# A decoder layer's merge and last feed forward: the squares, the first root and the first four weights of the feed forward made inside merge, whose last two blocks run chunk by chunk

## What is computed

```python
merged = jax.nn.sigmoid(ga) * (att @ w_branch_attn) + jax.nn.sigmoid(gr) * (rec @ w_branch_hgrn)
x = x + merged @ w_out
x = x + 0.5 * _swiglu(_rms_norm(x, ffn2_norm), ffn2_w_gate, ffn2_w_up, ffn2_w_down)
```

## Time and profile before

| | us |
|---|---|
| median of three runs | 3084.69 |
| the three runs | 3084.69, 3096.48, 3047.57 |
| the profiled execution | 3043.1 |
| its span, first to last instruction | 3041.4 |
| its mean granted TensorE clock | 0.959 |

### The profile page before, as it was taken

How to read it: one execution, slowest core, us unless ns; L and a number is a source line. 1 busy time by engine, 2 the same in 40 slices (tenths; PEclk the granted TensorE clock), 3 DMA queues, 4 the chain that set the end, 5 groups by cost and what they waited for, 6 DMA issues and landing times. The chain is left out here.

```text
span 3041.4 us, 50419 instructions
## 1 busy us (share of the span) xinstructions
PE 2893.8 (95%) x19265; PEld 2801.3 (92%) x19265; DVE 1496.7 (49%) x3238; ACT 701.6 (23%) x1354; POOL 578.4 (19%) x328
## 2 busy tenths in 40 slices
PE   8999999999799995999989989989989999999998
PEld 7999999999699983999968989979979999999998
DVE  5233322223677638999944656657344222333323
ACT  5111111111322225222213444431031111111111
POOL 0122122112221102222131121222002111221220
PEclk9999999999899998999999977889999999999999
DMA  4111111110223211233363142224211111111111
GB/s 128 42 44 61 47 41 55 41 41 21 97 58 96 72 51 44 91 132 114 104 168 87 44 157 69 87 92 144 56 49 56 42 41 41 41 59 51 41 34 58
DMA packets 239559, 213.04 MB, mean 70 GB/s; under 512 B 27106, under 2 KB 216834, under 8 KB 239298
## 3 DMA queue, kind: packets, MB, share of 16 engines
q1 hardware_dynamic: 229122, 180.85, 19.9%
q10 hardware_dynamic: 6336, 18.88, 1.6%
q0 software_dynamic: 3968, 11.54, 1.4%
HBM read 168.00 MB, written 43.21 MB: 69 GB/s over the span
## 5 line engine op out<-in xcount | busy, mean ns | idle before, releaser
L271 POOL TENSOR_TENSOR ff_wlo<-ff_raw,ff_whi 128x1024 fp32r<-128x1024 f32 x124 | 298.4, 2427 | 1203.8 <-ACT ff_whi L369 1202.5
L567 DVE TENSOR_TENSOR ff_prod<-ff_silu,ff_gu 128x384 f32<-128x384 f32 x132 | 68.7, 521 | 806.9 <-ACT ff_silu L374 806.9
L97 PE MATMUL ff_dn<-ff_ahi,ff_whi 128*128 128x384 f32 (+1 forms) x1056 | 341.0, 323 | 5.6 <-DVE ff_alo L573 3.8
L97 PE MATMUL ff_gu<-front_hhi,ff_whi 128*128 128x384 f32 (+1 forms) x1056 | 340.8, 323 | 1.8 <-DVE front_hlo L511 1.5
L98 PE MATMUL ff_dn<-ff_alo,ff_whi 128*128 128x384 f32 (+1 forms) x1056 | 339.7, 322 | 0.0
L99 PE MATMUL ff_dn<-ff_ahi,ff_wlo 128*128 128x384 f32 (+1 forms) x1056 | 339.6, 322 | 0.0
L99 PE MATMUL ff_gu<-front_hhi,ff_wlo 128*128 128x384 f32 (+1 forms) x1056 | 339.4, 321 | 0.0
L98 PE MATMUL ff_gu<-front_hlo,ff_whi 128*128 128x384 f32 (+1 forms) x1056 | 339.4, 321 | 0.0
L97 PE MATMUL ff_gu<-rear_hhi,ff_whi 128*128 128x384 f32 (+1 forms) x1056 | 338.8, 321 | 0.0
L98 PE MATMUL ff_gu<-rear_hlo,ff_whi 128*128 128x384 f32 (+1 forms) x1056 | 338.5, 321 | 0.0
L99 PE MATMUL ff_gu<-rear_hhi,ff_wlo 128*128 128x384 f32 (+1 forms) x1056 | 338.5, 321 | 0.0
(11 more groups left out here) (352 smaller groups left out, 6189.9 us busy)
## 6 DMA issues: line engine op xcount, KB each, us to landing
ff_raw<-in_ffn_w_gate SPq DMA_DIRECT2D x44, 512.0 KB, 3.7
ff_raw<-in_ffn_w_up SPq DMA_DIRECT2D x44, 512.0 KB, 3.7
ff_raw<-in_ffn_w_down SPq DMA_DIRECT2D x44, 512.0 KB, 3.5
scratch_feat<-sel_stage ACTq DMA_DIRECT2D x32, 528.0 KB, 2.7
sel_raw<-in_w_in SPq DMA_DIRECT2D x28, 512.0 KB, 3.6
merge_gates<-scratch_feat SPq DMA_DIRECT2D x48, 176.0 KB, 2.8
tok_raw<-in_w_in SPq DMA_DIRECT2D x8, 1024.0 KB, 6.6
mix_pages<-in_cache_k SPq DMA_DIRECT2D x52, 128.0 KB, 2.5
```

The lines of the kernel that those rows point to most:

```text
L97: nc.tensor.matmul(out, w_hi, x_hi, start=first, stop=False)
L271: nc.gpsimd.tensor_tensor(wlo[:, u, :], raw[:, u % RAW, :], whi[:, u, :], ALU.subtract).then_inc(w_lo_done, 1)
L567: nc.vector.tensor_tensor(prod[:, 0:w], act_out[:, b, 0:w], gu[:, b, 1, 0:w], ALU.mult).then_inc(prod_done, 1)
```

## The change

**Memory.** A new `EndRoom`, made before merge and kept through the feed forward, holds the sums of squares, the gain, and a large tile `branches`. Merge's high and low branch inputs lie in that tile; once the branch products are done, it holds the feed forward's weights and gate products.

**Merge.** After the gate products, SP loads the gain and, one after another, the first four gate and up weights into a part of the gates' room. ScalarE squares each block of `xT` after its additions (`square`), in its loop behind the conversion of the next weights, and then converts one of the four end weights (`end_hi`) in four of the steps. VectorE makes their low parts (`end_lo`). GpSimd adds the squares of blocks 1 to 5 to the sums (`gather`); block 0's squares are written straight into them. The loops of the second half are written out on ScalarE, VectorE and GpSimd. The last two blocks (6 and 7) are taken chunk by chunk: chunk 0 of both, chunk 1 of both, chunk 2 of both. Their squares are added by VectorE (`last_gather`). In front of the last product, TensorE multiplies the finished sums of the feed forward's first chunk with the ones (one product for what were eight), and the root of that chunk is made and refined beside the last product.

**The feed forward.** It starts with the scalings of chunk 0. Chunks 1 and 2 have one product with the ones each, ahead of sixteen idle products. Its loads begin with the fifth weight. The first feed forward (ff1) does the same work as before.

```diff
@@ -111,8 +111,31 @@
 LOGS = "natural_log_exp_and_others"
+class EndRoom:
+    def __init__(self, scope):
+        self.square_sums = scope.sb("square_sums", [P, T])
+        self.root = self.square_sums[:, 0:CHW]
+        self.branches = scope.sb("branches", [P, 16 * T], F32R, align=512)
+        self.gain = scope.sb("end_gain", [P, KD])
+        weights = self.branches[:, 0:12 * UNIT].rearrange("p (a b) -> p a b", b=UNIT)
+        self.whi, self.wlo = weights[:, 0:6, :], weights[:, 6:12, :]
+        a = self.branches[:, 12 * UNIT:12 * UNIT + 4 * TP].rearrange("p (a b) -> p a b", b=TP)
+        self.ahi, self.alo = a[:, 0:2, :], a[:, 2:4, :]
+        self.loaded, self.gain_in = scope.sem("end_loaded"), scope.sem("end_gain_in")
+        self.w_hi_done, self.w_lo_done = scope.sem("end_hi_done"), scope.sem("end_lo_done")
+def gate_or_up(w_gate, w_up, n, u):
+    return (w_gate, w_up)[u % 2][0].rearrange("(k p) f -> p k f", p=P)[:, :, DynSlice((2 * n + u // 2) * P, P)]
 def feed_forward(nc, tag, xT, hhi, hlo, gain, w_gate, w_up, w_down, ident, ones, x_in=None, gain_row=None, next_gain=None,
-                 y_out=None, constants=None, x_out=None):
+                 y_out=None, constants=None, x_out=None, given=None):
@@ -405,16 +434,9 @@
                         hi(0, 4)
                         hi(0, 5)
             else:
-                square(0)
-                inverse_root(0)
-                hi(0, 0)
-                square(1)
-                hi(0, 1)
                 h_hi(0)
-                hi(0, 2)
-                hi(0, 3)
+                nc.scalar.preload_act_table_set(LOGS)
                 inverse_root(1)
-                square(2)
                 h_hi(1)
                 inverse_root(2)
                 silu(0, 0)
@@ -602,20 +624,14 @@
                     for n in range(5 + 2 * q, 7 + 2 * q):
                         keep_y_lo(n)
             else:
-                variance(0)
-                lo(0)
                 dve.wait_ge(gain_in, 16)
-                refine(0)
                 for k in range(KD):
                     scale(0, k)
-                lo(1)
                 h_lo(0, 0)
                 h_lo(0, 1)
-                variance(1)
-                lo(2)
-                lo(3)
+                for e in range(S0, NCH):
+                    variance(e)
                 normalise(1)
-                variance(2)
                 product(0, 0)
                 normalise(2)
                 product(0, 1)
...
-                    pe.wait_ge(squared, KD * (e - E0) + k + 1)
-                    nc.tensor.matmul(out, ones[:, :], sq[:, k % 2, 0:w], start=(k == 0), stop=(k == KD - 1)
-                                     ).then_inc(summed, 1)
+                nc.tensor.matmul(dn[:, 1 + e, 0:w], ones[:, :], given.square_sums[:, cols(e)], start=True, stop=True
+                                 ).then_inc(summed, 1)
             def gate_up(i, q, between=None):
                 c, b = q // 2, q % 2
@@ -790,9 +801,9 @@
                 for q in range(3):
                     gate_up(0, q, rows_between)
             else:
-                idle_products(nc, gu[:, 1, 1, 0:P], ident, 10)
-                for e in range(NCH):
+                for e in range(S0, NCH):
                     sums(e)
+                idle_products(nc, gu[:, 1, 1, 0:P], ident, 16)
                 for q in range(3):
                     gate_up(0, q)
             for q in range(3, QS):
...
     RING = 3
     with Scope(nc, "merge") as s:
-        bhi = s.sb("bhi", [P, 8, T], F32R)
-        blo = s.sb("blo", [P, 8, T], F32R)
+        bhi = end.branches[:, 0:8 * T].rearrange("p (a b) -> p a b", b=T)
+        blo = end.branches[:, 8 * T:16 * T].rearrange("p (a b) -> p a b", b=T)
+        square_sums = end.square_sums
         mhi = s.sb("mhi", [P, KD, T], F32R)
         mlo = s.sb("mlo", [P, KD, T], F32R)
         whi = s.sb("whi", [P, 2, UNIT], F32R)
         wlo = s.sb("wlo", [P, 2, UNIT], F32R)
         branch = s.sb("branch", [P, RING, 2, CH])
-        gates = s.sb("gates", [P, 2, 2, CH])
-        both = s.sb("both", [P, 2, CH])
+        gates_room = s.sb("gates", [P, 3, CH])
@@ -2963,6 +2989,14 @@
                 for y in range(6):
                     load_gates(i, y)
+            sp.wait_ge(ps_done, 24)
+            sp.wait_ge(gated, 48)
+            sp.dma_start(end.gain[:, :], end_gain).then_inc(end.gain_in, 16)
+            for u in range(4):
+                if u:
+                    sp.wait_ge(end.w_lo_done, u)
+                sp.dma_start(end_raw.rearrange("p (k f) -> p k f", k=KD), gate_or_up(w_gate, w_up, 0, u)).then_inc(end.loaded, 16)
         @block.gpsimd
         def _(pool):
             s.clear_retired(pool)
...
                     else:
-                        pool.dma_start(raw[:, u, :].rearrange("p (k f) -> p k f", k=KD), wo[:, :, DynSlice((2 * i + u) * P, P)]
+                        pool.dma_start(raw[:, u, :].rearrange("p (k f) -> p k f", k=KD), wo[:, :, (2 * i + u) * P:(2 * i + u + 1) * P]
                                        ).then_inc(w_loaded[u], 16)
-            pairs(pool, body)
+                        if 2 * i + u >= 5:
+                            gather(2 * i + u - 4)
+            def gather(m):
+                for c in range(NCH):
+                    n = NCH * (m - 1) + c
+                    acc = square_sums[:, c * CH:(c + 1) * CH]
+                    pool.wait_ge(squared, n + NCH + 1)
+                    if n >= NCH:
+                        pool.wait_ge(gathered, n - NCH + 1)
+                    nc.gpsimd.tensor_tensor(acc, acc, squares[:, n % SQUARES, :], ALU.add).then_inc(gathered, 1)
+            body(0, 0, 0, True)
+            with pool.Fori(1, 4) as i:
+                body(0, i, i, False)
+            for i in range(4):
+                body(1, i, i + 4, False)
+            gather(4)
+            gather(5)
         @block.scalar
         def _(act):
             def hi(u):
                 nc.scalar.activation(whi[:, u, :], raw[:, u, :], ACT.Copy).then_inc(w_hi_done, 1)
+            def square(m):
+                for c in range(NCH):
+                    n = NCH * (m - 1) + c
+                    act.wait_ge(out_added, n + NCH + 1)
+                    if n >= SQUARES:
+                        act.wait_ge(gathered, n - SQUARES + 1)
+                    dst = squares[:, n % SQUARES, :] if m else square_sums[:, c * CH:(c + 1) * CH]
+                    nc.scalar.activation(dst, xT[:, m, c * CH:(c + 1) * CH], ACT.Square).then_inc(squared, 1)
+            def last_square(n):
+                act.wait_ge(out_added, 18 + n + 1)
+                act.wait_ge(gathered, 15)
+                nc.scalar.activation(squares[:, n, :], xT[:, KD - 2 + n % 2, n // 2 * CH:(n // 2 + 1) * CH], ACT.Square
+                                     ).then_inc(squared, 1)
+            def end_hi(u):
+                act.wait_ge(end.loaded, 16 * u + 16)
+                nc.scalar.activation(end.whi[:, u, :], end_raw, ACT.Copy).then_inc(end.w_hi_done, 1)
             for n, (c, j) in enumerate(parts):
                 act.wait_ge(branch_in[n % RING], 16 * (n // RING) + 16)
...
                 hi(u)
-            with act.Fori(1, 4) as i:
+            for i in range(1, 4):
                 for u in range(2):
                     act.wait_ge(w_loaded[u], 16 * i + 16 + 320)
                     act.wait_ge(out_done, 6 * i + 3 * u - 3)
                     hi(u)
+                    square(2 * i + u - 2)
+                    if 2 <= 2 * i + u - 1 < 6:
+                        end_hi(2 * i + u - 3)
+            for n in range(5):
+                last_square(n)
+            act.wait_ge(var_ready, 1)
+            act.wait_ge(last_gathered, 4)
+            nc.scalar.activation(root, var, ACT.Ln).then_inc(logged, 1)
+            act.wait_ge(logged, 1)
+            nc.scalar.activation(root, root, ACT.Exp, scale=-0.5).then_inc(rooted, 1)
+            last_square(5)
         @block.vector
         def _(dve):
...
                 nc.vector.tensor_tensor(x, x, out_ps[:, y % 3, 0:CH], ALU.add).then_inc(out_added, 1)
+            def last_add(n):
+                dve.wait_ge(out_done, 18 + n + 1)
+                x = xT[:, KD - 2 + n % 2, n // 2 * CH:(n // 2 + 1) * CH]
+                nc.vector.tensor_tensor(x, x, out_ps[:, n % 3, 0:CH], ALU.add).then_inc(out_added, 1)
+            def last_gather(n):
+                acc = square_sums[:, n // 2 * CH:(n // 2 + 1) * CH]
+                dve.wait_ge(gathered, 15)
+                dve.wait_ge(squared, 18 + n + 1)
+                if n % 2:
+                    dve.wait_ge(last_gathered, n)
+                nc.vector.tensor_tensor(acc, acc, squares[:, n, :], ALU.add).then_inc(last_gathered, 1)
+            def end_lo(u):
+                dve.wait_ge(end.w_hi_done, u + 1)
+                nc.vector.tensor_tensor(end.wlo[:, u, :], end_raw, end.whi[:, u, :], ALU.subtract
+                                        ).then_inc(end.w_lo_done, 1)
             def gates_of(i, u, first=False):
```

(71 more changed lines are left out.)

81 lines of the change are left out of this document (43 added, 38 removed).

## The result

The changed kernel's median is 3065.01 us (3060.91 to 3073.84, eight runs), that of the kernel before, eight runs by now, 3082.22 (3027.70 to 3096.48): 17 us less, and 3 from the forecast of 3062. The ratio of the runs that count as undisturbed is nevertheless 1.0078 (95% interval 1.005 to 1.0107), on the slower side of 1: it sets the three quick runs of before (3027.70, 3040.33, 3047.57) against all eight of after, among which there is no quick one.

A forecast was written before the change was run, and what follows sets the result against it. TensorE, busy 95% of the span, bounds the kernel, so its 32.7 us seam counts. Seam gain 23.5 less 1 for a later stall gives 22.5 us, off the shown median: 3062, range 3016 to 3080.

The forecast's parts named there:

- The seam: Between merge's last product and the feed forward's first: 9.2 us against 32.7, a gain of 23.5.
- the product with the ones: In front of merge's last product: one product in place of eight, taken at 0.5 us, at most 0.75.
- The tail: From merge's last product to the change of block: 2.5 us, 0.5 of it for the root; it was 0.9.
- What is late next: Feed forward's fourth product: VectorE's slack is 0.4 us and GpSimd's low parts fall on it; cost 1, between 0 and 3.
- rival C: Feed forward: the seam shrinks, but TensorE stalls as long for VectorE in the second to fourth product; 3082, chance 0.04.
- GpSimd's additions: In merge: 15 additions of squares, 0.84 us each, 12.6 in all; holds on VectorE between 0 and 0.84, taken as 0.
- The end weights: Four feed forward weights made in merge: each 1.07 on ScalarE, 1.22 on VectorE, load 3.7; slack 2.8 us, cost 0.
- rival B: In merge: waits for end weights' loads hold merge's own weights; at landings of 22 us 5 us slower, 3090; chance 0.03.
- The blocks chunk by chunk: Merge's last two blocks: block 7's weights needed 3.81 us after the first product starts; slack 1.3, cost 0, bounds 0 and 2.
- The clock in the seam: Between merge and feed forward: granted clock expected at 1.00 throughout, despite rests of about 2.5 and 1.3 us.
- rival A: In the seam: rests drop the clock to 1.2 GHz, losing 2.5 us and 1 more; gain 19, 3066; chance 0.18.
- Its bounds: For the whole gain: 25 us to 16 us; time range from 3016 to 3080.

The follow-up runs named there:

- e6: The changed kernel as in e3, but merge's last two blocks taken one after the other, product with the ones and root behind the last product: 3019.36 us.
- e3: The changed kernel with four idle products ahead of each of the recurrence's 36 groups of output products: 3015.96 us (four runs).
- e2: The kernel before with four idle products ahead of each of the recurrence's 36 groups of output products: 3037.84 us (ten runs).
- e5: e3 with the four end weights loaded, converted and split at the start of the feed forward again, not in merge: 3018.79 us.
- e7: e3 without the sixteen idle products at the start of the last feed forward: 3007.70 us (3005.71 to 3009.15).
- e1: The changed kernel again, no edit, beside the kernel before: 3044.10 us (six runs) against 3082.97, ratio 0.9886.
- e12: The kernel of e7 once more, beside e11: 3016.15 us (3008.71 to 3019.94, ten runs).
- e8: The changed kernel with one idle product ahead of each recurrence group: 3045.77 us (3016.05 to 3069.03, four runs).
- e9: The changed kernel a third time, no edit, beside the kernel before: 3066.76 us (12 runs) against 3080.25, ratio 0.9996.
- e4: The changed kernel with two idle products ahead of each recurrence group: 3014.07 us (3005.01 to 3016.84, four runs).
- e11: e3 once more, same kernel, beside e12: 3014.28 us (3013.73 to 3016.71).

## Why the prediction was right, and where it failed

**What the change does, it sized well.** Forecast: 22.5 us. Measured: 21.6 at a steady clock, 20 at equal clock, and 18 between the medians of all runs. Point by point:

- *The seam*: 9.2 forecast, of which 0.5 for the product with the ones. Measured 8.4, and 0.6 for that product in merge's output products (91.7 us before, 92.4 after, 91.7 in e6, where it is not among them): 9.0. The tail was 2.0, not 2.5, as the root was only 0.1 late; the 6.2 from the block's start to the first product was 6.3.
- *Merge's first half* has no term in the forecast. It took 1.4 us more after than before (112.3 against 110.9) and 2.1 more in e3 than in e2. Over all traces it is 110.3 to 114.4 us with the change (eleven) and 109.9 to 111.0 without (three). Whether the change costs this, and by what, is open. With it the stages of e2 and e3 give 24.7 - 0.6 - 2.1 = 22.0 us, as the totals do.
- *What is late next*, 1 us (0 to 3): nothing (rival C). The feed forward's 734.4 us are those of before (734.5). GpSimd's first low part starts at 2317.66, when chunk 2 was ready.
- *GpSimd's additions*: forecast at 0.84 each without cost. Alone they took 0.92 (2.75 for three), and beside VectorE's low parts 1.46, with the low part held too:

```profile
2263.68 1.23 DVE L3097 TENSOR_TENSOR merge_wlo<-join_w_raw,merge_whi 128x1024 fp32r<-128x1024 f32 x1 [0.63 <-ACT merge_whi L3037]
2264.82 1.97 DVE L3140 TENSOR_TENSOR rear_branches<-merge_gates,rear_branches 128x1024 fp32r<-128x1024 f32 x1
2266.72 0.51 DVE L3128 TENSOR_TENSOR rear_xT<-rear_xT,merge_out_ps 128x352 f32<-128x352 f32 x1
...
2264.11 4.39 POOL L3024 TENSOR_TENSOR rear_square_sums<-rear_square_sums,merge_branch 128x352 f32<-128x352 f32 x3 [7.05 <-ACT merge_branch L3047]
```

  The addition that follows starts at 2266.72, where its place in the beat of 3.82 us was 2266.34: 0.4 late, made up by the next one at 2270.16. The hold of the earlier trace rows is real and fell on slack, as argued. The Trainium skill, GPSIMD Engine Reference, Key points, names just this pair, a VectorE instruction with two SBUF inputs beside GpSimd; the 1.97 against 1.22 agrees. Rows 7 show more than such a pair: the slowed 2.21 is a cast with one input, which took 0.36 at 2293.09 without GpSimd beside it.
- *The end weights* (rival B): the slack was 1.3 us at the tightest, not 2.8. Beside GpSimd's own load the way from the issue to the conversion that waits for it was 5.6 us (2231.73 to 2237.37; 5.6 again from 2243.18), and 3.8 where SP's load was alone (from 2255.38), against the 3.7 of the forecast:

```profile
2231.73 0.37 SPq L2998 DMA_DIRECT2D merge_gates<-in_ffn_w_up  x1
...
2237.37 1.06 ACT L3058 ACTIVATE rear_branches<-merge_gates 128x1024 fp32r<-128x1024 f32 x1 [6.90 <-DMA merge_gates<-in_ffn_w_up]
2239.70 1.06 ACT L3037 ACTIVATE merge_whi<-join_w_raw 128x1024 fp32r<-128x1024 f32 x1 [1.26 <-PE merge_out_ps L99]
```

  Merge's conversion still waits for TensorE, not for the load. e5 shows what the part is worth: 3.8 us of seam and 1.6 behind it.
- *The blocks chunk by chunk*: worth 3.5 us (e6): 4.2 of seam, less the 0.6 of the product with the ones.
- *The clock in the seam* (rival A): the prediction wanted 1.00 throughout, and that was wrong. After the first rest, of 2.0 us, the clock fell in after (0.50 in 2288 to 2290), though not in e3. Rival A foresaw such a fall, at a price of 3.5 us. It cost next to nothing (a seam of 8.4 against 8.2 in e3), as the idle products took the loss:

```profile
2288.00:2290.00 2.00, 1.95 (x4) 1.23 (x5) 1.95 (x4) 0.00 (x0) 0.00 (x0) 0.50 0.47 131
2290.00:2292.00 2.00, 2.00 (x12) 1.85 (x11) 2.00 (x5) 1.48 (x1) 0.00 (x0) 0.65 0.99 369
2292.00:2294.00 2.00, 2.00 (x20) 2.00 (x19) 2.00 (x3) 1.58 (x2) 0.00 (x0) 1.00 0.90 270
```

  With them gone (e7) the fall costs 1.7 us. The Trainium skill, TensorE: Matmul & The Clock Gate, HAM oscillation, speaks of such gaps and of the clock lost behind them; e7 agrees, after shows that work without use can stand in for it.

- *Its bounds*: added up, its own terms give gains of 16.7 to 23.7 us, not 16 to 25, and the profiled execution less 25 is 3018, not 3016. Nothing here hangs on it.

**The step that failed** is that it let the rest of the kernel stand still. "All of the change lies in it or beside merge's output products in front of it", it says, takes the gain "off the median", and writes of the runs that they "lie at 3047.57, 3084.69 and 3096.48, 4 to 53 us above it, and none of that is in the seam as far as the trace tells". That is true and stopped short: the recurrence was put at nothing, without a reason. The runs show there a difference of more than twice the gain, with the same instructions: 49 us between the two profiled executions (249.2 to 298.3, clock 0.78 to 0.64), and 229 to 298 between four executions of the plain kernels. The trace of before had it already: its recurrence is at 0.78 of the clock, with some 110 us at half rate, and that share is drawn anew in each execution. The forecast thus set 22.5 us against a spread that it took as noise about one value, where runs lie near about five levels, for before 3022, 3044, 3065, 3082 and 3093, of which a few runs catch a few. A ratio from such runs can come out on either side of 1, and did. No rival named it: A looked for the clock in the seam alone.

So it was in part luck that the first median came within 3 us of 3062: both medians of eight runs fell on low levels. The median of e1's six runs was 3044, 18 away.

**Not settled**: what draws the level. Some sets lie together (all of e7 within 4 us, all eight first runs of after within 13), while the same programs lay elsewhere or wider in another session (e12, e1). The three sessions of experiments ran on three chips, but that alone does not set the level: on each of them before's runs cover at least 3031 to 3095. No run here tells whether it comes from the moment at which the recurrence starts or from something else.

**A better version**: the change with two idle products in each group of the recurrence, 3014.07 (3005.01 to 3016.84), ratio to the kernel before 0.982 (0.975 to 0.990); with four, 3014.9 over eight runs. Against the changed kernel's own median of 3063.9 that is 50 us, more than twice what the change brings. It is no floor: the two quickest plain executions of the changed kernel took 3001.8 and 3001.9.

## What to carry to other kernels

Before a gain of 1% is set against a median, find out in which stage the runs differ: compare each stage's granted clock and instruction count, not its busy share. If a stage that the change doesn't touch draws its clock anew, hold the clock there in both kernels, or compare runs of equal clock; 12 runs of the plain kernel, by their ratio, could not tell the sign; eight against ten with a steadied clock gave the size within 3 us. Work of other engines that was moved beside merge's output products cost TensorE nothing there, as long as the slack of each queue was counted one instruction at a time, down to 1.3 us.

## What was not expected of the hardware

TensorE stayed at 1.2 GHz (a granted clock of 0.50) from 1900 to 2080 in after while it was busy 172 of those 180 us by the trace, mostly with matmuls of 64 and 128 columns. Four idle products of 128 columns ahead of each group brought the mean clock of the stage from 0.64 to 0.87 up to 0.90 to 0.97, and the added work paid at the median (3082 to 3038, and 3064 to 3015), though not against the quickest plain executions. The same rest of 2.0 us at the start of the feed forward was followed by a fall of the clock in the traces of after, e1, e8 and e9 and by none in e3, e4 and e11; one of 3.1 us was followed by none.
